# A streaming encoder step on one core: where TensorE's four attention blocks stand among the dense products of a slot

## The chip, the core and the metric

One core of a Trainium2 chip runs the whole program in one launch. The number is device time in microseconds (us), the median of three executions; a separate execution was profiled. Engines: PE is TensorE (PEld its weight loads), DVE VectorE, ACT ScalarE, POOL GpSimd, SP SyncE, which issues most of the DMAs.

## The reference

A two-layer encoder step for 1024 new frames and 64 frames of a running stream (512 past frames in a cache), width 1024, all in float32. Layer 0 projects to stick-breaking attention heads and gated spatial groups, mixes them with one output projection, and runs a SwiGLU; layer 1 has a state-space mixer, a GLU and another SwiGLU. The attention of one head is what the change touches:

```
z = einsum('bqhd,bkhd->bhqk', q, k) * HEAD_DIM**-0.5
mask = k_pos < q_pos
log_stay  = where(mask, log_sigmoid(-z), 0)
log_after = cumsum(log_stay, over keys, reverse) - log_stay
w   = where(mask, exp(log_sigmoid(z) + log_after), 0)
out = einsum('bhqk,bkhd->bqhd', w, v)
...
x = x + concat(out, gated) @ w_out
x = x + (silu(h @ w_gate) * (h @ w_up)) @ w_down
```

## The kernel before

Every dense operand is split into a high and a low part, so that a **product** is three matmuls (`three`, L248: lines 251, 252, 253) into one PSUM bank. The part of the program around the change runs from about 380 to 1000 us of the span. It is a list of **slots** (`SLOTS`, planned at L1076 to L1162). A slot holds dense groups and at most one or two **units** of attention, and each engine walks the list in order (`mid_pe`, `mid_dve`, `mid_act`, `mid_pool`, `mid_sp`).

There are 68 units. A unit is a pair of heads, one block of 128 keys and up to 512 queries: units 0 to 15 are the first 512 frames (128, 256, 384, 512 queries for the four key blocks of each head pair), units 16 to 67 the second 512 frames and the 64 running ones (per pair of heads 128, 256, 384, five times 512, then five of 64). The last unit of a group of queries has no remaining sums. PE does four things for attention:

- **sums** of unit i (`at_sums` with `tri`, L982): the running sum over keys within the block, four matmuls, after softplus and its remainder are there;
- **scores** of unit i + 3 (L970 to L974), four matmuls, two more on a diagonal block;
- **values** of unit i - 1 (L994), which read the exponent; two float32 matmuls that the trace shows as four passes;
- **remaining sums** of unit i (`at_sums` with `comp`, L982), which complete the sum for the next block of keys; they wait until DVE has subtracted the sums.

Before, a slot's PE order is sums, scores, values, in a row (`at_pe`), then half of the dense work, the remaining sums (`at_pe_rest`), and the other half.

DVE has three steps per unit: **t** (L922) subtracts the sums of unit i from its scores; **c** (L931) copies the scores of unit i + 3 out of PSUM; **s** (L939) forms the softplus of unit i + 2 and a rounding (L943) writes its high part. POOL then writes the remainder, **splo** (L955). ACT takes the exponent of unit i (L888), then three activations on the scores of unit i + 3 (L911, L913, L915) for the softplus. The buffer `tz` has four places, so c waits for the values of unit i - 1 (LEAD is 3):

```
def at_dve_c(dve, i):
    c = i + LEAD
    ...
    dve.wait_ge(sem("u_z"), c + 1)
    if c >= 4:
        dve.wait_ge(sem("u_pv"), c - 3)
    dve.tensor_copy(tz[:, c % 4, :, 0:w], ps[:, 3:5, 0:w])
```

In `mid_dve` the order in a slot is t, c, s, then the evictions of the dense groups; with four groups, t, first eviction, c, second eviction, s, the other two. Evictions are: for an up product a multiplication (L1354) and a rounding rh (L1358), after which POOL writes the remainder rl (L1325); for down, outS and outA products an addition to the residual (L1364). A gate product is evicted by ACT with silu (L1279). ACT also rounds the weight slabs (L241), POOL subtracts their remainder (L245). Dense groups use three PSUM banks in turn, so a group waits until the group three before it has been evicted (`used`).

The slots with attention are, in order: three without products that only start the pipeline; eight with one outS group of four products (units 0 to 7); nine with no product (units 8 to 16); eight with one outA group of four products (units 17 to 25); three for a norm (units 26 to 28); then the feed-forward, where a slot holds one gate group or one up group of eight products, or four down groups of two products each, in the order gate, up, gate, up, down, down (units 29 to 67). The running stream's units of 64 queries come two to a slot; the first of the two is done whole before the slot's dense work.

SP's queue holds the weight slabs and, in `at_loads` (L797), the keys, queries and values of later units, which wait for counts of scores (`u_z`) and values (`u_pv`).

Of the kernel before, what the change touches and what calls it, by code (L numbers as in the profile page):

```python
# [76 lines left out]
def build(nc, A, O):  # L77
    with ExitStack() as ctx:
        sems = {}

        def sem(name):
            if name not in sems:
                sems[name] = ctx.enter_context(nc.semaphore(name))
            return sems[name]
# [6 lines left out]
        def plan(off, *specs):  # L91

            got = []
            for name, shape, dt in specs:
                n = 4
                for s in shape[1:]:
# [16 lines left out]
        xin, nrow, _ = plan(off_g, ("xin", [P, 2, D], F32), ("nrow", [P, P], F32))  # L113
# [6 lines left out]
        ug0, _ = plan(off_end, ("ug0", [P, T], F32))  # L120
        wsr, _ = plan(off_end, ("wsr", [P, 8, P], F32))
        g4, _ = plan(off_end + T * 4, ("g4", [P, 2, GP, 4], F32))
        zhi, _ = plan(off_end, ("zhi", [P, T], F32R))
# [3 lines left out]
        zlo, _ = plan(off_g + 8 * P * 4, ("zlo", [P, T], F32R))  # L127
# [9 lines left out]
        splo, _ = plan(off_x + 4 * (2 * KCOL + 4 * 576 + 13 * P), ("splo", [P, 4, 2, 512], F32R))  # L137
# [4 lines left out]
        hA, lA, _, rh, rl, xA, mst, oa = plan(  # L142
            off_h, ("hA", [P, KD * 512], F32R), ("lA", [P, KD * 512], F32R), ("hpad", [P, 512], F32), ("rh", [P, 3, 576], F32R),
            ("rl", [P, 3, 576], F32R), ("xA", [P, KD * 512], F32), ("mst", [P, 2, 576], F32))
# [7 lines left out]
        eb, bo, co_, pb, _ = plan(off_x, ("eb", [P, 2, 8, NCH], F32), ("bo", [P, 8, 2, P], F32), ("co", [P, 8, 2, CW], F32),  # L152
                                  ("pb", [P, 2, GP, L], F32))
        zt, chi, clo, _ = plan(_, ("zt", [P, 512], F32), ("chi", [P, 512], F32R), ("clo", [P, 512], F32R))
# [5 lines left out]
        t1, t2, _ = plan(off_t, ("t1", [P, 8 * CW], F32), ("t2", [P, 8 * CW], F32))  # L160
        assert _ <= off_end
        lt, craw, lstep, _ = plan(off_t, ("lt", [P, 5, P], F32), ("craw", [P, 2, 8, 64], F32), ("lstep", [P, 2], F32))
# [6 lines left out]
        tm, kt, p4, _ = plan(off_w + 6 * D * 4, ("tm", [P, 2, 8, P], F32), ("kt", [P, 8, P], F32), ("p4", [P, 5, GP], F32))  # L169
        u, ca, sh, oa = plan(off_g, ("u", [P, 2, 8, NCH], F32), ("ca", [P, 3, 4, 2, CW], F32), ("sh", [P, 2, 2, 4, NCH], F32))  # L170
        assert oa <= off_end
        yp, _ = plan(off_h + KD * T * 4, ("yp", [P, KD * T], F32))
# [7 lines left out]
        hp, _ = plan(off_h, ("hp", [P, KD * T], F32))  # L180
        fin, fout, _ = plan(off_w - 2 * D * 4 - 3072, ("fin", [P, 4, GP], F32), ("fout", [P, 4, P], F32))
        sq, _ = plan(off_g, ("sq", [P, 6, 384], F32))
        ssum, _ = plan(off_end, ("ssum", [P, NC, 384], F32))

        yf, _ = plan(off_h, ("yf", [P, KD * T], F32))
        yo, _ = plan(off_g, ("yo", [P, 2, D], F32))
# [552 lines left out]
        NU = len(units)  # L739
# [237 lines left out]
        def at_sums(pe, i, mat):  # L977
            u, w = units[i], units[i]["w"]
            for a in range(2):
                out = ps[:, 5 + a, u["off"]:u["off"] + w]  # L980
                for j, r in enumerate((sphi[:, i % 2, a, 0:w], splo[:, i % 4, a, 0:w])):
                    mm = pe.matmul(out, mat[:], r, start=mat is tri and u["first"] and j == 0, stop=True, skip_group_check=True)  # L982
            return mm

        def at_values(pe, i):
            u, g = units[i], group_no[i]
            pe.wait_ge(sem("u_w"), i + 1)
            if u["first"]:
                v_ready(pe, i)
                if g:  # L990
                    o_taken(pe, g - 1)
            for a in range(2):
                out = ps[64 * a:64 * a + 64, 7, u["off"]:u["off"] + u["w"]]
                mm = pe.matmul(out, vv[:, u["vb"], 64 * a:64 * a + 64], tz[:, i % 4, a, 0:u["w"]],  # L994
                               start=u["first"], stop=True, skip_group_check=True)
            mm.then_inc(sem("u_pv"), 1)

        def at_pe(pe, i):
            if 0 <= i < NU:
                pe.wait_ge(sem("u_splo"), i + 1)  # L1000
                if units[i]["first"] and i:
                    pe.wait_ge(sem("u_t"), i)
                at_sums(pe, i, tri).then_inc(sem("u_tri"), 1)
            if i + LEAD < NU:
                at_scores(pe, i + LEAD)
            if 1 <= i <= NU:
                at_values(pe, i - 1)

        def at_pe_rest(pe, i):
            if 0 <= i < NU and not units[i]["last"]:  # L1010
                pe.wait_ge(sem("u_t"), i + 1)
                at_sums(pe, i, comp).then_inc(sem("u_rest"), 1)

        G, USES, SRC, SLOTS = [], {"a": 0, "v": 0}, [], []
        NORMS = [(1, 0, 0), (1, 1, 0), (1, 1, 1), (2, 0, 0), (2, 1, 0), (2, 1, 1)]
# [59 lines left out]
        for j in range(4):  # L1079
            t = slab(w_out[:, 4:8, 2 * j * P:2 * (j + 1) * P])  # L1080
            for m in (2 * j, 2 * j + 1):
                g = group("outS", 0, 0, m, [t])
# [3 lines left out]
        for j in range(4):  # L1086
            t = slab(w_out[:, 0:4, 2 * j * P:2 * (j + 1) * P])
            for m in (2 * j, 2 * j + 1):
                g = group("outA", 0, 0, m, [t])
                new_slot([g], some_steps(), sq=squares([g], (1, 0)))  # L1090
        g = group("rms", 0, 0, 0, [])
# [313 lines left out]
                        row = 8 + f  # L1405
                    dve.scalar_tensor_tensor(out, xf, cols[:, row:row + 1], rf, ALU.mult, ALU.mult).then_inc(sem("m_f"), 1)

        def dense_pe(pe, g, halfway=None):

            v = G[g]  # L1410
            kind, half, m, n, s = v["kind"], v["half"], v["m"], v["n"], v["s"]
            if g >= 3:
                used(pe, g - 3)
            out = ps[:, v["bank"], 0:n]
            for t in v["slabs"]:
                if g == min(h for h in range(max(0, g - 16), g + 1) if t in G[h]["slabs"]):
                    pe.wait_ge(sem("w_lo"), t + 1)
            if kind == "rms":
                q = rms_group.index(g)
                pe.wait_ge(sem("m_add"), q_adds[q])  # L1420
                if half == 0 and NORMS[q][0] == 1:
                    pe.wait_ge(sem("consts"), 1)
                pe.matmul(out, ones[:], msum[:, q % 2, 0:n], start=True, stop=True).then_inc(sem("g_ready"), 1)
                return
            if kind == "down":
                pe.wait_ge(sem("hid_lo"), hid_no[(half, 2 * (m_part[g]) + 1, v["c"])] + 1)
                count = 2
            else:
                count = 4 if kind in ("outS", "outA") else KD
            for j in range(count):  # L1430
                if halfway is not None and j == count // 2:
                    halfway()
                if kind == "down":
                    b = tile_no(half, 2 * m_part[g] + j) % 3
                    o = s - HALF[half][0]
                    r1, r2 = rh[:, b, o:o + n], rl[:, b, o:o + n]
                    t, col = v["slabs"][j], m * P
                else:
                    t = v["slabs"][0]
                    k, col = j, j * P  # L1440
                    if kind in ("outS", "outA"):
                        k, col = (4 + j if kind == "outS" else j), j * 256 + (m % 2) * P
                        if kind == "outS" and m == 0:
                            pe.wait_ge(sem("ms_lo"), j + 1)
                        elif kind == "outA" and m == 0:
                            pe.wait_ge(sem("o_lo"), j + 1)
                    elif kind == "outB":
                        k = (j + 4) % KD
                        col = k * P
                        if m == 0:  # L1450
                            pe.wait_ge(sem("ms_lo"), 4 + j + 1)
                    elif kind == "gate" and m == 0:
                        q = NORMS.index((1, half, v["c"]))
                        pe.wait_ge(sem("m_lo"), KD * q + j + 1)
                    r = cols_of(half, k, s, n)
                    r1, r2 = hh[half][:, r], hl[half][:, r]
                mm = three(pe, out, slot(t), col, r1, r2, j == 0, j == count - 1)
            mm.then_inc(sem("g_ready"), 1)
# [8 lines left out]
        def mid_pe(pe):  # L1467
            pe.wait_ge(sem("at_made"), 4)
            pe.wait_ge(sem("acc_used"), NC * IN_TILES)
            pe.wait_ge(sem("kv_used"), kv_taken(len(TOKS)))  # L1470
            for S in SLOTS:
                gs, at = S["groups"], S["at"]
                for i in at[:-1]:
                    at_pe(pe, i)
                    at_pe_rest(pe, i)
                for i in at[-1:]:
                    at_pe(pe, i)
                for n, g in enumerate(gs):
                    if at and len(gs) == 1:
                        dense_pe(pe, g, lambda: at_pe_rest(pe, at[-1]))  # L1480
                        continue
                    if at and n == len(gs) // 2:
                        at_pe_rest(pe, at[-1])
                    dense_pe(pe, g)
                if at and not gs:
                    at_pe_rest(pe, at[-1])

        def prep_sp(sp):  # L1490
# [890 lines left out]
```

## Time and profile before

| | us |
|---|---|
| median of three runs (lowest, highest) | 2809.38 (2804.43, 2810.51) |
| profiled execution | 2812.7 |
| its span, first to last instruction | 2810.9 |
| PE busy | 2565.4 (91% of the span) |
| PE weight loads busy | 2364.7 (84%) |
| DVE, ACT, POOL busy | 1166.2, 881.3, 1104.3 |

The mean granted TensorE clock was 0.941 of 2.4 GHz; its two levels are 1.2 and 2.4 GHz. The chain of work that ended last is PE for 75% of the span, DVE for 9%. A matmul's end is modelled, so its duration is longer than its share of PE's time: the pace is read from one start to the next. Idle time stands in brackets behind an instruction, with what ended it.

### The profile page before, as it was taken

To read this page: it belongs to the slowest core of one execution; us is meant where nothing else is said; L and a number is where in the kernel's file an instruction comes from. 1 tells how busy PE (TensorE), PEld (TensorE's weight loads), DVE (VectorE), ACT (ScalarE), POOL (GpSimd) and SP (SyncE) were. 2 spreads that over 40 slices of the span, in tenths; PEclk is the share of its full clock that TensorE was granted. 3 is DMA by queue.
4 is the path that set the end of the run, shared out by engine and by line. 5 is a ranking of instruction groups with operands and counts; after the bars stand their busy time and mean duration, and the time that the engine had idled before them with its cause. 6 is when DMAs were issued, how large, how long until landed. Compare 5 with 4: busy or idle time off the path is not lost.

```text
span 2810.9 us, 38283 instructions
## 1 busy us (share of the span) xinstructions
PE 2565.4 (91%) x15274; PEld 2364.7 (84%) x15274; DVE 1166.2 (41%) x1877; ACT 881.3 (31%) x1304; POOL 1104.3 (39%) x770
## 2 busy tenths in 40 slices
PE   6998949899997999999999587799699999999998
PEld 4898936677776978999999466799699999999998
DVE  3696637765562232422223677322412222222224
ACT  3423236788882322211221121311311111111114
POOL 2545534564454565544444200333532222222223
PEclk9999969899998999999999677899899999999999
DMA  4315664323423223322222675311011111111111
GB/s 121 103 59 198 243 200 115 86 72 82 110 72 123 83 83 98 106 83 90 76 84 68 170 195 149 126 46 46 29 40 44 41 42 44 45 45 45 45 45 64
DMA packets 290436, 254.11 MB, mean 90 GB/s; under 512 B 32561, under 2 KB 254705, under 8 KB 289025
## 3 DMA queue, kind: packets, MB, share of 16 engines
q1 hardware_dynamic: 282064, 219.96, 27.3%
q0 software_dynamic: 7088, 31.15, 2.9%
q8 instruction: 91, 1.49, 0.2%
q10 hardware_dynamic: 1152, 1.18, 0.1%
q14 instruction: 41, 0.33, 0.0%
HBM read 195.08 MB, written 54.80 MB: 89 GB/s over the span
## 4 chain that ended last, share of the span: by engine, by line
PE 75%; DVE 9%; DMA 5%; POOL 4%; ACT 2%; issue 2%; SPq 1%; POOLq 0%; DVEq 0%; ACTq 0%
PE ps L251 22%; PE ps L252 22%; PE ps L253 22%; PE ps L982 3%; PE ps L1870 1%; PE ps L994 1%; DVE v L1932 1%; DMA mst<-mT 1%; DVE fbuf L423 1%; PE ps L1868 1%; POOL hlo L431 1%; PE ps L974 1%; DVE t L1707 1%; POOL ssum L349 1%; PE ps L970 1%
## 5 line engine op out<-in xcount | busy, mean ns | idle before, releaser
L245 POOL TENSOR_TENSOR wlo<-raw,whi 128x1024 fp32r<-128x1024 f32 x250 | 602.8, 2420 | 402.1 <-ACT whi L241 400.4
L251 PE MATMUL ps<-hhi,whi 128*128 128x384 f32 (+1 forms) x1920 | 635.8, 331 | 49.0 <-POOL hlo L2019 14.9
L252 PE MATMUL ps<-hlo,whi 128*128 128x384 f32 (+1 forms) x1920 | 631.3, 329 | 0.0
L253 PE MATMUL ps<-hhi,wlo 128*128 128x384 f32 (+1 forms) x1920 | 631.1, 329 | 0.0
L251 PEld LDWEIGHTS ps<-hhi,whi 128*128 128x128 f32 x1920 | 365.2, 190 | 54.8 <-issue 22.5
L252 PEld LDWEIGHTS ps<-hlo,whi 128*128 128x128 f32 x1920 | 365.3, 190 | 0.3 <-issue 0.2
L253 PEld LDWEIGHTS ps<-hhi,wlo 128*128 128x128 f32 x1920 | 364.9, 190 | 0.0
L241 ACT ACTIVATE whi<-raw 128x1024 fp32r<-128x1024 f32 x250 | 259.1, 1054 | 312.9 <-PE ps L253 145.6
L251 PE MATMUL ps<-hB,whi 128*128 128x288 f32 x832 | 247.3, 297 | 12.3 <-POOL lB L1316 12.3
L509 POOL TENSOR_TENSOR gl<-fbuf,gh 128x384 f32 (+3 forms) x66 | 63.9, 968 | 488.8 <-DVE gh L564 488.8
L253 PE MATMUL ps<-hB,wlo 128*128 128x288 f32 x832 | 246.4, 296 | 0.0
L252 PE MATMUL ps<-lB,whi 128*128 128x288 f32 x832 | 246.2, 296 | 0.0
L561 DVE TENSOR_TENSOR fbuf<-ps,abuf 128x384 f32<-128x384 f32 (+1 forms) x66 | 35.4, 536 | 452.5 <-ACT abuf L479 448.2
L479 ACT ACTIVATE abuf<-ps 128x384 f32<-128x384 f32 (+1 forms) x66 | 31.1, 473 | 559.8 <-PE ps L253 559.8
L251 PE MATMUL ps<-rh,whi 128*128 128x288 f32 (+1 forms) x528 | 177.4, 336 | 14.7 <-DVE xA L1364 6.4
L572 DVE TENSOR_TENSOR x<-ps,x 128x384 f32<-128x384 f32 (+1 forms) x264 | 141.3, 535 | 109.9 <-PE ps L253 108.7
L1354 DVE TENSOR_TENSOR fb<-ps,ab 128x288 f32<-128x288 f32 (+1 forms) x66 | 35.3, 536 | 365.2 <-PE ps L253 342.2
L252 PE MATMUL ps<-rl,whi 128*128 128x288 f32 (+1 forms) x528 | 175.0, 332 | 0.0
L253 PE MATMUL ps<-rh,wlo 128*128 128x288 f32 (+1 forms) x528 | 174.8, 331 | 0.0
L253 PE MATMUL ps<-gh,wlo 128*128 (+2 forms) x528 | 172.1, 326 | 0.0
L252 PE MATMUL ps<-gl,whi 128*128 (+2 forms) x528 | 172.0, 326 | 0.0
L251 PE MATMUL ps<-gh,whi 128*128 (+2 forms) x528 | 172.0, 326 | 0.0
(315 smaller groups left out, 4796.6 us busy)
## 6 DMA issues: line engine op xcount, KB each, us to landing
raw<-in_ffn_w_gate SPq DMA_DIRECT2D x66, 512.0 KB, 3.8
raw<-in_ffn_w_up SPq DMA_DIRECT2D x66, 512.0 KB, 3.9
raw<-in_ffn_w_down SPq DMA_DIRECT2D x66, 512.0 KB, 3.6
raw<-in_ab_w_in SPq DMA_DIRECT2D x20, 512.0 KB, 4.1
raw<-in_ab_w_out SPq DMA_DIRECT2D x16, 512.0 KB, 3.8
raw<-in_ssm_w_glu SPq DMA_DIRECT2D x16, 512.0 KB, 3.9
dC<-co POOLq DMA_DIRECT2D x4, 1152.0 KB, 4.7
ca<-dC SPq DMA_DIRECT2D x8, 576.0 KB, 4.9
```

Of the source, the lines that this page charges most:

```text
L241: act.activation(whi[:, slot(t), :], raw[:, t % 2, :], ACT.Copy).then_inc(sem("w_hi"), 1)
L245: pool.tensor_tensor(wlo[:, slot(t), :], raw[:, t % 2, :], whi[:, slot(t), :].bitcast(F32), ALU.subtract).then_inc(sem("w_lo"), 1)
L251: pe.matmul(out, wh, rh, start=first, stop=False)
L252: pe.matmul(out, wh, rl, start=False, stop=False)
L253: return pe.matmul(out, wl, rh, start=False, stop=last)
L349: pool.tensor_tensor(ssum[:, c, 0:n], ssum[:, c, 0:n], sqbuf(k, a)[:, 0:n], ALU.add).then_inc(sem("n_add"), 1)
L479: act.activation(abuf[:, v % 2, 0:n], ps[:, 2 * (v % 2), 0:n], ACT.Silu).then_inc(sem("pair_act"), 1)
L509: pool.tensor_tensor(gl[:, bass.ds(o, n)], fbuf[:, v % 2, 0:n], gh[:, bass.ds(o, n)].bitcast(F32), ALU.subtract).then_inc(sem("hid_lo"), 1)
L561: dve.tensor_tensor(fbuf[:, v % 2, 0:n], ps[:, 2 * (v % 2) + 1, 0:n], abuf[:, v % 2, 0:n], ALU.mult).then_inc(sem("pair_used"), 1)
L572: dve.tensor_tensor(xo, acc(v)[:, 0:n], xo, ALU.add).then_inc(sem("acc_used"), 1)
L982: mm = pe.matmul(out, mat[:], r, start=mat is tri and u["first"] and j == 0, stop=True, skip_group_check=True)
L1354: dve.tensor_tensor(fb2[:, h % 2, 0:n], out, ab2[:, h % 2, 0:n], ALU.mult).then_inc(sem("use_v"), 1)
```

## The change

In a slot PE does the sums, two dense products, the scores, two products, the remaining sums, two products, the values, two products. `at_pe` becomes a generator that stops twice after each block; `dense_pe` lets it go on once before each product, so a block comes before every second product. In a unit without remaining sums the values come before the fifth product. In a slot with four products the remaining sums and the values come one after the other behind the last product; in a slot without products, and for the first unit of two in a slot, the order is sums, scores, remaining sums, values with nothing between. No other engine's order is changed.

```
         def at_pe(pe, i):
+
             if 0 <= i < NU:
                 pe.wait_ge(sem("u_splo"), i + 1)
                 if units[i]["first"] and i:
                     pe.wait_ge(sem("u_t"), i)
                 at_sums(pe, i, tri).then_inc(sem("u_tri"), 1)
+                yield
+                yield
             if i + LEAD < NU:
                 at_scores(pe, i + LEAD)
-            if 1 <= i <= NU:
-                at_values(pe, i - 1)
-
-        def at_pe_rest(pe, i):
+                yield
+                yield
             if 0 <= i < NU and not units[i]["last"]:
                 pe.wait_ge(sem("u_t"), i + 1)
                 at_sums(pe, i, comp).then_inc(sem("u_rest"), 1)
+                yield
+                yield
+            if 1 <= i <= NU:
+                at_values(pe, i - 1)
...
-        def dense_pe(pe, g, halfway=None):
+        def dense_pe(pe, g, side):
...
             for j in range(count):
-                if halfway is not None and j == count // 2:
-                    halfway()
+                next(side, None)
...
             for S in SLOTS:
                 gs, at = S["groups"], S["at"]
                 for i in at[:-1]:
-                    at_pe(pe, i)
-                    at_pe_rest(pe, i)
-                for i in at[-1:]:
-                    at_pe(pe, i)
-                for n, g in enumerate(gs):
-                    if at and len(gs) == 1:
-                        dense_pe(pe, g, lambda: at_pe_rest(pe, at[-1]))
-                        continue
-                    if at and n == len(gs) // 2:
-                        at_pe_rest(pe, at[-1])
-                    dense_pe(pe, g)
-                if at and not gs:
-                    at_pe_rest(pe, at[-1])
-
+                    for _ in at_pe(pe, i):
+                        pass
+                side = at_pe(pe, at[-1]) if at else iter(())
+                for g in gs:
+                    dense_pe(pe, g, side)
+                for _ in side:
+                    pass
```

## Rows read from the trace of the kernel before

**Rows 1.** Stretches: us; busy (count) of PE, PEld, DVE, ACT, POOL; clock; DMA

```profile
458.00:493.00 35.00, 29.44 (x158) 20.45 (x157) 26.28 (x37) 26.48 (x39) 15.91 (x10) 0.95 0.53 118
493.00:540.00 47.00, 45.76 (x221) 33.38 (x222) 39.01 (x44) 33.32 (x45) 30.51 (x18) 1.00 0.35 85
...
575.00:860.00 285.00, 282.43 (x1373) 220.90 (x1372) 167.40 (x210) 243.91 (x281) 142.00 (x81) 0.98 0.32 87
```

**Rows 2.** Timeline of PE, unit 46's slot: start, us, engine, line, operation, count

```profile
704.74 0.39 PE L982 MATMUL ps<-sphi,tri 128*128 128x512 f32 x1
...
705.64 0.39 PE L970 MATMUL ps<-qS,kS 128*128 128x512 f32 x1
...
706.64 1.08 PE L994 MATMUL ps<-tz,vv 128*64 128x512 f32 x4
707.65 0.50 PE L251 MATMUL ps<-hA,whi 128*128 128x512 f32 x1
...
710.51 0.39 PE L982 MATMUL ps<-sphi,comp 128*128 128x512 f32 x1
...
714.13 0.39 PE L982 MATMUL ps<-sphi,tri 128*128 128x512 f32 x1
```

**Rows 3.** Timeline of DVE, the same slot

```profile
705.84 1.22 DVE L922 TENSOR_TENSOR tz<-tz,ps 128x1024 f32<-128x1024 f32 x1 [2.86 <-PE ps L982]
707.84 1.23 DVE L931 COPY tz<-ps 128x1024 f32<-128x1024 f32 x1 [0.77 <-PE ps L994]
...
711.68 0.69 DVE L943 CAST sphi<-esp 128x1024 fp32r<-128x1024 f32 x1 [0.24 <-PE ps L982]
...
715.12 0.43 DVE L1358 CAST rh<-fb 128x512 fp32r<-128x512 f32 x1
```

**Rows 4.** Waits, 380 to 880: who <- whom: us in total, times, longest

```profile
DVE tz L931 <- PE ps L994: 32.8, 44, 2.4
...
PE ps L994 <- ACT tz L888: 2.1, 2, 1.3
```

**Rows 5.** Timeline of DVE, 598 to 604

```profile
599.64 1.22 DVE L939 SCALAR_TENSOR_TENSOR esp<-tz,esp 128x1024 f32<-128x1024 f32 x1
```

**Rows 6.** DVE by line and shape, 380 to 880: count, busy us, mean ns, idle before

```profile
L939 DVE SCALAR_TENSOR_TENSOR esp<-tz,esp 128x1024 f32<-128x1024 f32 x24 | 42.7, 1781 | 0.1
...
L943 DVE CAST sphi<-esp 128x1024 fp32r<-128x1024 f32 x24 | 22.0, 918 | 10.3 <-PE ps L982 9.9
...
L931 DVE COPY tz<-ps 128x128 f32<-128x128 f32 x20 | 5.8, 288 | 6.5 <-PE ps L994 6.5
```

**Rows 7.** Timeline of all engines, 587.1 to 588.2, an up slot (unit 30)

```profile
587.16 2.40 POOL L955 TENSOR_TENSOR splo<-esp,sphi 128x1024 fp32r<-128x1024 f32 x1 [0.63 <-DVE sphi L943]
...
587.23 0.69 DVE L1354 TENSOR_TENSOR fb<-ps,ab 128x512 f32<-128x512 f32 x1
...
587.96 1.88 DVE L1358 CAST rh<-fb 128x512 fp32r<-128x512 f32 x1
```

**Rows 8.** Timeline of ACT, unit 46's slot

```profile
710.16 1.05 ACT L911 ACTIVATE esp<-tz 128x1024 f32<-128x1024 f32 x1
...
713.62 1.06 ACT L915 ACTIVATE esp<-esp 128x1024 f32<-128x1024 f32 x1
```

**Rows 9.** Timeline of PE, unit 17's slot

```profile
496.06 0.44 PE L994 MATMUL ps<-tz,vv 128*64 128x128 f32 x4 [0.97 <-DVE lA L948]
```

**Rows 10.** Timeline of PE, units 39 and 40, two to a slot

```profile
649.96 0.19 PE L982 MATMUL ps<-sphi,tri 128*128 128x64 f32 x1
...
654.55 0.48 PE L994 MATMUL ps<-tz,vv 128*64 128x64 f32 x4 [1.32 <-ACT tz L888]
654.97 0.80 PE L251 MATMUL ps<-hA,whi 128*128 128x512 f32 x1
```

**Rows 11.** Stretches of 4 us, columns as in rows 1

```profile
652.00:656.00 4.00, 2.68 (x18) 2.18 (x18) 1.39 (x4) 3.92 (x6) 2.76 (x2) 0.72 0.00 0
656.00:660.00 4.00, 4.00 (x11) 3.14 (x10) 0.43 (x1) 3.91 (x7) 0.00 (x0) 0.50 0.75 223
```

## Prediction

> **What bounds the kernel now.** I read the busy time by stretch first [rows 1]. From 575 to 860 us, where nearly every slot carries eight dense products beside attention, TensorE (PE) is busy 282.4 of 285.0 us at a granted clock of 0.98; ScalarE (ACT) has 243.9, VectorE (DVE) 167.4. From 493 to 540, with four products a slot, PE has 45.8 of 47; from 458 to 493, with none, 29.4 of 35. PE runs in program order, so whatever it waits in these slots is added to the end. Then one slot at full width, unit 46, on PE [rows 2]: sums at 704.74, scores 705.64, values 706.64, first product 707.65, remaining sums 710.51, next slot 714.13. That is 9.39 us, without a wait: blocks of four 512-column matmuls take 0.90 (0.225 each), values 1.01, a dense product (three matmuls) 0.68. Then the same slot on DVE [rows 3]: the subtraction t starts at 705.84, when the sums are done. The copy c of unit 49's scores starts at 707.84, 1.20 after the values started, because it overwrites the buffer of four that the values of unit 45 read. Over the stage that wait occurs 44 times and makes 32.8 us of DVE idle [rows 4]. It harms nothing, since it falls early in the slot.
>
> **The change, part by part.** No instruction is added or removed; the matmuls, weight loads and waits are the same. The sums stay first. The scores move back by two products (1.36 us); their reader c now waits for something later anyway: 0. The remaining sums come 4.5 us into the slot (0.90 + 1.36 + 0.90 + 1.36) in place of 5.8, so t has 1.3 us less. The values go from 1.9 us into the slot to 6.8, behind six products. This last is the costly part: c (unit i+3) waits for them, and behind c in DVE's order are softplus s and the rounding of unit i+2, evictions, and t of unit i+1, for which PE's remaining sums of i+1 wait. A loop closes once per slot, with V the start of the values.
>
> PE from V to the next remaining sums, full width: values 1.01 + two products 1.47 (the first of six matmuls costs 0.11 more, 707.65 behind values) + sums 0.90 + 1.36 + scores 0.90 + 1.36 = 7.0 us. A narrower unit (384, 256, 128, 64 columns) takes less in proportion, an estimate.
>
> DVE from V to the end of t: values seen 1.20, c 1.23, s, rounding, evictions, t 1.22. For s the trace has two prices: 1.22 with GpSimd (POOL) idle [rows 5] and 1.78 in the mean [rows 6]; for the rounding 0.69 [rows 3] and 0.92 in the mean [rows 6]. I take 1.91 for the two together, the free ones, since POOL's weight subtraction would mostly fall before s, and keep 2.70 as the upper end. 64-column units take 0.29 for c [rows 6].
> - Slot with a gate product: nothing else. 1.20 + 1.23 + 1.91 + 1.22 = 5.6, covered by 7.0: 0.
> - Slot with an up product: the product's multiplication (0.69 [rows 7]) and its rounding rh (0.43 [rows 3]) now come before t, right when POOL starts splo. There rh took 1.88 instead of 0.43 and ended 0.3 us after splo's 2.40 [rows 7], so 2.7 us from rounding to t. Before s, ACT's silu of the gate slot delays POOL by about 0.5 (my estimate from ACT's chain of 4.5 us [rows 8] plus silu, slab and POOL's turn). Sum 1.20 + 1.23 + 0.5 + 1.91 + 2.7 + 1.22 = 8.8, that is 1.7 us of stall. With each unit's own widths: units 30, 32, 34, 42, 46, 56, 60: 1.5, 1.6, 1.1, 0.6, 1.7, 1.5, 1.1 = **9.1**. Below: 0 (no meeting with POOL); above: 15 (the mean prices, 0.8 more in each).
> - Slot with four down products: one eviction (0.69) before s, two after. Bank reuse makes the next slot's products wait for these too. Units 43, 44, 57, 58: 1.0, 0.6, 0.9, 0.6 = **3.1** (5.7 with 2.70).
> - First units of two-unit slots have nothing between sums and remaining sums; behind down slots (units 52, 65) DVE is 1.1 late: **2.2**.
> - Slots with outA and four products (units 17 to 21): PE from V only 5.6, DVE 6.3: 0.5, 0.6, 0.6, 0.7, 0.1 = 2.5 with the free prices, 6.2 with the mean ones (0.8 more on each of four or five). POOL is busier there than behind (30.5 of 47 us against 142 of 285 [rows 1]), so I take a value between, **4.0**.
> - Slots with outS: only unit 4, between full and narrow units, is late, 1.2, and a little on unit 5: **1.5**.
> - Nine slots without products (units 8 to 16): values now follow the remaining sums, which follow t, so c starts up to 1.6 us later. Carried along DVE's order this is about 1.75 per four units: **4.0**. Right behind them, in unit 17's slot, PE waits 0.97 before the values of unit 16 [rows 9]; products now stand before them, which gives back **1.0**.
>
> What it gives: in the two-unit slot at 650 us narrow matmuls run 5 us without a product, the last 1.32 of them a wait for the exponent [rows 10]; with one more such wait it is 2.1 us [rows 4]. In the two stretches of 4 us from 652 the granted clock is 0.72 and 0.50 [rows 11]: the 1.2 GHz level for 2.2 + 4.0 us, so 3.1 us of work lost. After the change products stand in that run, and I take both as gone: **-5.2**.
>
> Sum: 9.1 + 3.1 + 2.2 + 4.0 + 1.5 + 4.0 - 1.0 - 5.2 = +17.7 us.
>
> Costed at nothing: SyncE's queue. Its loads of keys and values wait for counts of scores and values, which come up to 5 us later; weight slabs queue behind them. What hides it: these rows are needed four slots later and a slab is two slots ahead; without that cover, up to 5 us at each of some eight places. ACT: its chain starts with c, 4 us later, and is needed only at the next slot's s: 9.4 against 4.5 [rows 8].
>
> The Trainium skill (SBUF — State Buffer, Who interferes with whom) says VectorE's two-input operations and its 2-port casts share a port pair with GpSimd, held for a whole instruction. It speaks against this change, which brings rh beside splo in every up slot; by it the up slots pay their 9.1. The 587.96 row agrees, but it is the plainest of few; without interference they would pay 0, and the sum would be +8.6.
>
> **How the time stands.** The profiled execution took 2812.7 us (span 2810.9); the three runs' median is 2809.4, 3.3 below. +17.7 gives 2830.4 for an execution like it and 2827.1, said **2827**, at the median.
>
> **Rivals.**
> (a) Covered: the loop is shorter than PE's path nearly everywhere (s and rh free of POOL, t in time); up slots cost 0 and the other losses half, 6.7 (3.1, 2.2, 2.5, 1.5 and 4.0), against gains of 6.2. For it: gate slots have 1.4 us to spare. Against: the down and the product-less slots don't depend on POOL. +0.5: about 2810.
> (b) Faster, the other side: the point is whether DVE's chain stays under 7.0 us in full-width slots and is absorbed in the product-less ones. If so, only the waits before values and the 1.2 GHz stretch go, -5.2 and -1.0: about 2803. Against it: c's wait is a real one in 44 places, and moves 4.9 us back.
> (c) Wholly bound by DVE: s and roundings meet POOL in most slots. Up 15, down 5.7, outA 6.2, the rest as above, and PE in the product-less slots, already at the lower clock for part of them (0.95 in the stretch [rows 1]), falls there for longer, doubling about 1 us of remaining sums and values on the loop in some six slots: 15 + 5.7 + 6.2 + 2.2 + 1.5 + 4.0 + 6 - 6.2 = +34, about 2844.
> (d) That interleaving itself speeds PE, small weight loads hiding behind dense matmuls. Each block that gains at its entry loses at its exit, where a dense load stands behind a narrow matmul; I count it 0 and give it no chance of its own.
>
> **How the numbers follow.** Forecast 0.62 (2816 to 2838), (a) 0.14, (b) 0.07, (c) 0.17. The range of 8 in 10 reaches into (a) and (c): 2810 to 2845. Differences under 0.2% (5.6 us) can't be told from none by measurement. Faster by more is (b), 0.07; within it is (a), 0.14; slower is the forecast and (c), 0.79.
>
> **What would show it.** DVE's c should start about 1.2 us behind the values at three quarters of the slot, with its idle for values well above 32.8 us; PE should have waits before the remaining sums on t (L922) in slots behind up and down products, none behind gates; rh (L1358) should have a mean near 2 us while attention runs; the clock near 655 us should stay at the upper level. The stage from the first sums (412 us) to the last values (855 us) should be some 17 us longer, and everything behind it only shifted. Wrong I would be if PE showed no new wait on DVE (then (a) or (b)), or if the loss stood at slab loads.

## The result and the profile after

| | before | after |
|---|---|---|
| median (lowest to highest), us | 2809.95 (2804.43 to 2812.79) | 2846.68 (2841.24 to 2853.71) |
| profiled execution, its span | 2812.7, 2810.9 | 2843.5, 2841.8 |
| DVE, ACT, POOL busy | 1166.2, 881.3, 1104.3 | 1148.1, 882.6, 1102.4 |
| mean granted clock | 0.941 | 0.936 |

Over four executions of each the ratio is 1.0135 [1.0105, 1.0164]: **slower by 36.7 us**, where 17.7 were forecast and 2845 was the upper end of the range. The sign was right, the size was half, and the range missed by 1.7 us. PE, DVE, ACT and POOL are busy for about as long as before: the time lies in waits and in TensorE's clock.

The waits first, 380 to 920 us of after (who waits, for whom: us in total, times, longest). The first line answers [rows 4]:

```profile
DVE tz L931 <- PE ps L994: 184.2, 63, 5.7
...
PE ps L982 <- DVE tz L922: 34.3, 24, 6.9
...
PE ps L982 <- POOL wlo L245: 1.9, 1, 1.9
```

The copy c waited 32.8 us for the values before; now it waits 184.2, in nearly every slot. The second line is where PE pays for it: before the sums or remaining sums it waits for t, 24 times and 34.3 us. In the same stretch of before it was

```profile
PE ps L982 <- DVE tz L922: 10.2, 4, 6.2
```

so that 24.1 us of the loss stand as waits on t; the rest are smaller waits and the lower clock below. The place shows in unit 46's slot, on PE (start, us, engine, line, operation), which answers [rows 2]:

```profile
727.41 0.39 PE L982 MATMUL ps<-sphi,tri 128*128 128x512 f32 x1
...
729.68 0.39 PE L970 MATMUL ps<-qS,kS 128*128 128x512 f32 x1
...
731.95 0.39 PE L982 MATMUL ps<-sphi,comp 128*128 128x512 f32 x1
...
734.31 1.08 PE L994 MATMUL ps<-tz,vv 128*64 128x512 f32 x4
...
736.81 0.39 PE L982 MATMUL ps<-sphi,tri 128*128 128x512 f32 x1
...
742.97 0.50 PE L982 MATMUL ps<-sphi,comp 128*128 128x512 f32 x1 [1.66 <-DVE tz L922]
```

and on DVE, which answers [rows 3]:

```profile
735.51 1.23 DVE L931 COPY tz<-ps 128x1024 f32<-128x1024 f32 x1 [5.18 <-PE ps L994]
736.65 1.66 DVE L939 SCALAR_TENSOR_TENSOR esp<-tz,esp 128x1024 f32<-128x1024 f32 x1
738.34 0.69 DVE L943 CAST sphi<-esp 128x1024 fp32r<-128x1024 f32 x1
...
739.67 2.12 DVE L1359 CAST rh<-fb 128x512 fp32r<-128x512 f32 x1
741.71 1.21 DVE L922 TENSOR_TENSOR tz<-tz,ps 128x1024 f32<-128x1024 f32 x1
```

The slot's four blocks start 2.27, 2.27 and 2.36 us apart, as predicted (0.90 and 1.36, the values a little later). From the values (734.31) to the next slot's remaining sums (742.97) are 8.66 us, of which PE's own work is 7.0. On DVE c starts 1.20 behind the values, then s, the rounding, the up product's two evictions and t follow without a gap. That is the loop: values, c, s, rounding, evictions, t, remaining sums, and values again.

The stretches of after (us; busy time and count of PE, PEld, DVE, ACT, POOL; clock; DMA), shifted by what went before, stand against [rows 1] and [rows 11]:

```profile
466.40:476.40 10.00, 9.14 (x30) 6.80 (x31) 4.78 (x8) 3.62 (x8) 3.60 (x3) 0.50 1.06 244
...
501.00:548.00 47.00, 43.72 (x196) 29.88 (x194) 31.47 (x37) 30.43 (x39) 27.57 (x15) 1.00 0.29 72
...
590.00:896.00 306.00, 288.97 (x1377) 217.50 (x1376) 157.83 (x210) 244.60 (x281) 141.74 (x80) 0.98 0.30 81
...
609.80:613.20 3.40, 3.40 (x11) 2.39 (x10) 0.00 (x0) 1.04 (x2) 2.29 (x1) 0.52 0.05 5
...
676.00:680.00 4.00, 4.00 (x27) 3.51 (x27) 1.04 (x4) 3.97 (x4) 1.09 (x1) 1.00 0.00 0
```

The third line is the feed-forward: its 285 us have become 306, with 17 us of PE idle instead of 2.6. The second, with four products a slot, has PE busy 43.7 of 47 us instead of 45.8. The first line is in the slots without products: ten microseconds at the 1.2 GHz level, where before it was low for about 3.5 (0.95 in the mean of 35 [rows 1]). The fourth is a new stretch of 3.4 us at that level, in the slot of unit 31. The last is the two-unit slot that stood at 0.72 and 0.50 before: full clock now, as forecast.

To place the loss I took each unit's first sums in both traces and subtracted. The difference is -1.3 us at unit 0, -1.4 at unit 8, +7.4 at 17, 5.8 at 18, 10.8 at 24, 14.7 at 29, 24.7 at 39, 20.6 at 41, 31.5 at 61, and 36.0 at the last values: 37.3 from first to last. The stage was expected to be some 17 us longer, with everything behind it only shifted. The end of the span is 30.9 late, since what lies behind attention came out 5.1 shorter in this trace; in the traces of the kernels below it varies likewise, and I tested nothing there.

### The profile page after: what moved, and what is told of

It reads as the page before. It is cut to its first block, busy times and chain, and to the rows that moved or that the text cites. A ratio compares the mean times of both kernels' runs of the same rounds, so it can differ in the third digit from the quotient of the medians.

```text
span 2841.8 us, 38291 instructions
## 1 busy us (share of the span) xinstructions
PE 2575.3 (91%) x15274; PEld 2361.4 (83%) x15274; DVE 1148.1 (40%) x1877; ACT 882.6 (31%) x1304; POOL 1102.4 (39%) x770
## 4 chain that ended last, share of the span: by engine, by line
PE 73%; DVE 12%; DMA 5%; POOL 4%; issue 3%; ACT 2%; SPq 1%; POOLq 0%; DVEq 0%; ACTq 0%
PE ps L251 21%; PE ps L253 21%; PE ps L252 21%; PE ps L982 3%; PE ps L994 2%; PE ps L1863 1%; DVE v L1925 1%; DVE esp L939 1%; DMA mst<-mT 1%; DVE fbuf L423 1%; PE ps L1861 1%; POOL hlo L431 1%; DVE hp L1407 1%; DVE t L1700 1%; POOL ssum L349 1%
```

## The experiments

The theory: moving the values late makes c, and with it all of DVE's work behind c, part of a loop that closes once per slot through the reuse of `tz`. The rivals: the loss lies in the interleaving itself (switches between narrow and dense matmuls cost PE, the opposite of (d)); or in TensorE's clock in the slots without products. In all that follows "shift" is the start of a unit's sums, less that of before's trace.

**A fifth place for tz.** Everything of after stays; a fifth buffer, in a place that is free by then, makes c of unit i+3 wait for the values of unit i-2, one slot earlier. The control is the same edit on before.

```diff
+        def tzb(i):
+            return tz4[:] if i % 5 == 4 else tz[:, i % 5, :, :]
...
-                if c >= 4:
-                    dve.wait_ge(sem("u_pv"), c - 3)
-                dve.tensor_copy(tz[:, c % 4, :, 0:w], ps[:, 3:5, 0:w]).then_inc(sem("u_c"), 1)
+                if c == 4:
+                    dve.wait_ge(sem("ms_lo"), 4)
+                if c >= 5:
+                    dve.wait_ge(sem("u_pv"), c - 4)
+                dve.tensor_copy(tzb(c)[:, :, 0:w], ps[:, 3:5, 0:w]).then_inc(sem("u_c"), 1)
```

Every other use of tz takes its place from `tzb` too; the wait at c = 4 is for the mixer, which uses the fifth place earlier.

> The changed kernel with a fifth place for the scores buffer tz (4 KB that the mixer's staging buffer leaves free while attention runs), so that the copy c of unit i+3 waits for the values of unit i-2, done a slot before, and no longer for those of unit i-1; PE's order stays the changed one. Theory, the loop through c: the waits of PE on t in front of the remaining sums behind up and down products go, and so does the longer stretch without products; what is left is the gain (the 1.2 GHz stretch near 655 us, the waits for the exponent): about 2803 us, between 2797 and 2810. Rival, that standing between products itself costs PE (weight loads, waits at more block boundaries): still above 2830. In between, near 2820, both have a part.

Measured: 2810.08 us over 12 runs, ratio to before 1.0001 [0.9986, 1.0016]. The whole loss is gone, with after's PE order unchanged, so that the rival of a cost in the interleaving itself falls. Its waits, 380 to 920 us (in this kernel t is L926, c L937, the sums L988, the scores L980):

```profile
DVE tz L937 <- PE ps L980: 44.3, 44, 4.3
...
PE ps L988 <- DVE tz L926: 16.5, 10, 5.8
```

c waits for the scores, not for the values, and PE's waits for t fall from 34.3 us to 16.5. The expected 2803 (2797 to 2810) was just missed on the slow side: the gain near unit 40 is there (the shift falls by 4.1), but behind it the shift grows by 4.6 again, 1.4 of it at unit 57, where PE waits 1.25 us for a weight slab, and 1.6 from unit 63 to 67, in the two-unit slots; from unit 0 to the last values 1.1 of gain is left in this trace.

> The kernel before with the same fifth place. Control: both theories say that c's wait (32.8 us of DVE idle) is hidden in the old order, so the time stays at 2810 within 4 us. If it falls by more than 6, c's wait also cost something before, and what the fifth place brings to the changed kernel is not the undoing of the change alone.

Measured: 2805.02 us over 12 runs, 0.9991 [0.998, 1.0001]. With the old order the fifth place is worth nothing that can be measured. c's wait, 32.8 us in sum before, was hidden, as the prediction said of it; moved, it was not.

**Only the values back at their old place.** Sums, two products, scores and values, two products, remaining sums, four products.

```diff
             if i + LEAD < NU:
                 at_scores(pe, i + LEAD)
-                yield
-                yield
+            if 1 <= i <= NU:
+                at_values(pe, i - 1)
+            if i + LEAD < NU or 1 <= i <= NU:
+                yield
+                yield
...
-            if 1 <= i <= NU:
-                at_values(pe, i - 1)
```

> The changed kernel with the values put right behind the scores (sums, two products, scores and values, two products, remaining sums, four products). Buffers as before. Theory: c starts some 4 us earlier in the slot, DVE has 11.9 us from the values to the next remaining sums in place of 7.0, more than its longest chain (8.8 to 10): no wait of PE on t, about 2805 us (2800 to 2812). Rival of the boundaries: scores and sums still stand apart, so at least half of the loss stays, above 2825.

Measured: 2804.8 us over 10 runs, 0.999 [0.9977, 1.0002]. The waits:

```profile
DVE tz L931 <- PE ps L994: 70.8, 54, 2.6
...
PE ps L982 <- DVE tz L922: 9.3, 3, 6.2
```

c still waits for values, twice as long as before in sum, but early in the slot, and PE's waits for t are those of before. The other separations together cost nothing. Of the shift, 5.5 us are gained in this trace, 3.9 of them near unit 40; over all runs the gain is inside the uncertainty.

**Only the values moved.** Sums and scores in a row, four products, remaining sums, two products, values, two products.

```diff
                 at_sums(pe, i, tri).then_inc(sem("u_tri"), 1)
-                yield
-                yield
             if i + LEAD < NU:
                 at_scores(pe, i + LEAD)
+            if 0 <= i < NU or i + LEAD < NU:
+                yield
+                yield
                 yield
                 yield
```

> The other half alone: sums and scores in a row as in the kernel before, four products, remaining sums, two products, values, two products. Theory: DVE has the same 7.0 us from the values to the next remaining sums, so nearly all of the loss is there: about 2842 us (2832 to 2852). Rival of the boundaries: one block less stands apart, 2825 or less; if the scores' place mattered, close to 2810.

Measured: 2855.26 us, 1.0164 [1.0146, 1.0183], above the 2832 to 2852 that I gave it. The whole loss is in the values' move, and by this order some 8 us more than by after's in the medians, though the two intervals overlap. In the traces the extra is 6.7 us and lies ahead of the feed-forward: from unit 0 to unit 26 the shift grows by 20.9 where after's grows by 14.5. Why, no run shows.

**The values one product later still.**

```diff
                 at_sums(pe, i, comp).then_inc(sem("u_rest"), 1)
                 yield
                 yield
+                yield
```

> The changed kernel with the values one product later (behind the seventh in place of the sixth, in units with remaining sums and slots of eight products). Theory: PE's way from the values to the next remaining sums is one product (0.68 us) shorter and DVE's chain the same, so every slot in which PE waits on t pays 0.68 more: eleven in the feed-forward, +7.5, about 2854 us (2850 to 2859), and slots behind gates still pay nothing (5.6 against 6.3). Rival, that the loss is not this loop: within 3 us of 2847.

Measured: 2865.55 us, 1.0215 [1.0195, 1.0234]: 0.80% above after's ratio, some 22 us, where 7.5 were expected. The sign follows the theory; the total doesn't. The profiled execution was the fastest of the four, and its trace holds 13.7 us more than after's from unit 0 to the last values. The other three were not traced. The price of one wait came out as expected: each of PE's five waits on t behind up slots is 0.67 to 0.71 us longer than in after, where 0.68 was worked out. For unit 47 it is, in after and here,

```profile
742.97 0.50 PE L982 MATMUL ps<-sphi,comp 128*128 128x512 f32 x1 [1.66 <-DVE tz L922]
750.39 0.65 PE L982 MATMUL ps<-sphi,comp 128*128 128x512 f32 x1 [2.33 <-DVE tz L922]
```

Yet behind the up slots of units 46 and 60 the shift grows by 4.3 and 4.6 us instead of 2.1 and 2.5. Three of six stretches of the feed-forward at the lower clock in this kernel's trace (columns as before) show the rest of why, as far as this trace goes:

```profile
655.00:658.40 3.40, 3.40 (x10) 2.64 (x9) 0.00 (x0) 0.12 (x1) 1.58 (x1) 0.50 1.03 225
750.60:753.80 3.20, 3.20 (x8) 2.45 (x8) 0.00 (x0) 1.67 (x2) 2.29 (x1) 0.50 0.01 3
...
870.00:873.40 3.40, 2.95 (x7) 2.37 (x8) 0.39 (x1) 1.06 (x1) 2.96 (x2) 0.51 0.00 0
```

After has two such stretches there (609.8 and 811.2). With longer stalls the granted clock falls behind more of them, and then the work that follows is slower too: 3.4 us at half clock are 1.7 us more, so the four more are 6.8 us, beside the 7.5 worked out. The length of the wait alone doesn't decide: in after the wait of 2.14 us before 651.49 left the clock at full speed,

```profile
651.60:655.00 3.40, 3.40 (x15) 1.90 (x15) 0.34 (x1) 0.84 (x1) 2.32 (x1) 1.00 1.04 240
```

and so did one of 2.09 (856.65), while one of 1.87 (810.63) did not. What decides, no run shows.

**Evictions ahead of s.** In up slots DVE does the multiplication and rh between c and s, so that rh no longer runs beside splo.

```diff
                 if not at or len(gs) < 4:
                     cut1 = cut2 = 0
+                if at and [G[g]["kind"] for g in gs] == ["up"]:
+                    cut2 = 1
```

> The changed kernel, but in a slot with an up product DVE evicts that product (multiplication and rounding rh) between c and s, no longer behind s. PE's order and all waits stay. Theory: what made the up slots dear is the meeting with POOL, rh with splo (2.65 us from the rounding to t) and s with the weight remainder (s 2.7 to 3.1 us in four of the seven full-width up slots). With rh 3 us after the values start and s behind it, both are free: the chain from values to t falls from 8.6 to 9.9 to about 7.3, so 7 slots give back 1.3 to 2.5 each: 2847 - 13 = 2834 (2828 to 2840). Rival, that DVE's bare work is too long whoever meets whom: 2843 or more, because the order within DVE does not change the sum.

Measured: 2839.38 us, 1.0101 [1.0082, 1.012], inside the 2828 to 2840 around the 2834 expected. Its interval overlaps after's, so the gain is read from the traces: from unit 0 to the last values the shift grows by 26.7 us instead of 37.3. This kernel's waits and unit 46's slot on DVE:

```profile
PE ps L982 <- DVE tz L922: 23.8, 21, 6.9
```

```profile
731.28 1.23 DVE L931 COPY tz<-ps 128x1024 f32<-128x1024 f32 x1 [5.19 <-PE ps L994]
732.84 0.69 DVE L1355 TENSOR_TENSOR fb<-ps,ab 128x512 f32<-128x512 f32 x1 [0.34 <-PE ps L253]
733.57 0.43 DVE L1359 CAST rh<-fb 128x512 fp32r<-128x512 f32 x1
733.91 1.22 DVE L939 SCALAR_TENSOR_TENSOR esp<-tz,esp 128x1024 f32<-128x1024 f32 x1
...
735.77 1.22 DVE L922 TENSOR_TENSOR tz<-tz,ps 128x1024 f32<-128x1024 f32 x1
```

The instructions are the same as in after, but rh takes 0.43 instead of 2.12 and s 1.22 instead of 1.66. t ends 6.9 us behind the values (730.08 in this trace), inside PE's 7.0. The growth of the shift behind units 30, 32, 34, 46 and 60 falls from 4.6, 2.0, 2.5, 2.1, 2.5 to 0.2, 0.1, 0.7, 0.4, 0.6. So in these up slots it is the meeting with POOL that decides. The 2.0 and 2.2 between units 56 and 58 stay, and the early part stays.

**The new order only in slots of eight products.** All slots ahead of the feed-forward, and first units of two, keep the old order (`at_pe_old`).

```diff
+        def at_pe_old(pe, i):
...
-                    for _ in at_pe(pe, i):
+                    for _ in at_pe_old(pe, i):
...
+                eight = sum(2 if G[g]["kind"] == "down" else 8 if G[g]["kind"] in ("gate", "up") else 0 for g in gs) == 8
-                side = at_pe(pe, at[-1]) if at else iter(())
+                side = (at_pe if eight else at_pe_old)(pe, at[-1]) if at else iter(())
```

> The changed order only in slots with eight products (units 29 on); in slots with four or none, and for the first unit of a two-unit slot, the order of the kernel before. Theory by the shift from trace to trace: units 0 to 26 lost 12 to 14 us of the 37 (8.8 in the slots without products, 5.0 in the outA slots), so about 2833 (2828 to 2838). If the half of the clock lost in the slots without products were the main thing, more would return: 2825 or less.

Measured: 2827.85 us, 1.0067 [1.005, 1.0084]. The feed-forward's part is about 18.8 us, the other half, 17.9, lies ahead of it, where the shift is now flat between 2.1 and 2.6 up to unit 31. I had expected a little more from the feed-forward (2828 to 2838). PE waits for t 20.9 us in 9 places:

```profile
PE ps L982 <- DVE tz L922: 20.9, 9, 6.2
```

**Matmuls without use in the slots without products.** Four of 512 columns into an unused bank, between the scores and the remaining sums of units 8 to 16, to hold the clock up. They only add work.

```diff
+            if 8 <= i <= 16:
+                if i == 8:
+                    used(pe, 7)
+                for _ in range(4):
+                    pe.matmul(ps[:, 0, :], identr[:], hA[:, 4 * 512:5 * 512], start=True, stop=True)
             if 0 <= i < NU and not units[i]["last"]:
                 pe.wait_ge(sem("u_t"), i + 1)
```

> The changed kernel with four 512-column matmuls of no use between the scores and the remaining sums in the nine slots without products (units 8 to 16), where PE stands 0.8 to 2.9 us for t. They add 3.6 us of work per four units, the more part of it in idle time. If the lower clock there (13.4 us at 1.2 GHz in the changed kernel, 3.5 before) makes the stretch longer, the clock stays up and the shift over units 8 to 17, 8.8 us in the changed kernel, falls to 7 or less, the total by 1 to 3 us. If the order alone makes it, the shift stays at 8.8 or grows by up to 2.

Measured: 2850.85 us, 1.0155 [1.0136, 1.0174]. The stretches of this kernel (columns as before):

```profile
466.00:476.00 10.00, 7.36 (x42) 5.32 (x40) 7.29 (x9) 6.40 (x9) 5.58 (x3) 1.00 0.68 165
466.00:493.00 27.00, 22.26 (x122) 15.70 (x120) 18.09 (x26) 17.64 (x25) 10.16 (x6) 1.00 0.66 154
```

The clock stays at 2.4 GHz through all of it, and still the shift grows by 8.7 us from unit 8 to unit 17, against 8.8 in after. The lower clock isn't what that stretch can be won back by. It isn't excluded as a part: the added matmuls are 0.9 us a slot, and what they cost and what the clock gave are not told apart.

**Both remedies together.** Values at their old place, and five places for tz (the first and the second diff).

> Both remedies together: values right behind the scores, and the fifth place for tz. By the traces of the two alone, the values' place gives 5.5 us by the end of attention, nearly all in the two-unit slot near 650 us, and the fifth place under the old order 3.4 us in the slots without products: if they add up, 2807 - 8 = 2799 us (2796 to 2803), faster than both kernels. If the fifth place brings nothing once the values come early, 2804.

Measured: 2803.27 us over 12 runs, 0.9987 [0.9973, 1.0], the lowest median of all, but no gain that can be told from none; 2799 was expected. In the traces, from unit 0 to the last values, the shift falls by 6.4 us here, by 5.5 in values_second and 3.4 in five_before: the two gains add only in part.

## Why the prediction was half right

In the table, in us, the growth of the shift over the units of each term.

| term | predicted | measured |
|---|---|---|
| outS, units 0 to 8 | +1.5 | -0.1 |
| slots without products, 8 to 17 | +4.0 | +8.8 |
| given back at unit 17 | -1.0 | -1.6 |
| outA, 18 to 24 | +4.0 | +5.0 |
| last outA and norm slots, 24 to 29 | 0 | +3.9 |
| up slots: behind 30, 32, 34, 42, 46, 60 | +7.6 | +14.6 |
| behind the up slot of 56, and the weight slab late at unit 57 | +1.5 | +4.2 |
| down slots: behind 43, 44, 57, 58 | +3.1 | +2.2 |
| two-unit slots | +2.2 | +3.1 |
| wait for the exponent and clock, near unit 40 | -5.2 | -4.1 |
| not placed | | +1.3 |

The sum failed by the size of its terms: the up slots above all, the slots without products, and two terms put at nothing, the slots of units 24 to 29 and the late slab.

**The mechanism** was right in the main: c starts 1.20 behind the values, PE has new waits on t of 1.66 to 2.79 us behind the up slots of units 30, 32, 34, 46 and 60 and none behind gates, the lower clock near 655 us goes. Behind the down slots of units 43, 44, 57 and 58 the forecast had PE wait for t and for the banks of the dense groups; only the second is there, 0.4 us before the sums of the next unit, for an eviction:

```profile
718.11 0.50 PE L982 MATMUL ps<-sphi,tri 128*128 128x512 f32 x1 [0.40 <-DVE xA L1365]
```

five_after and values_second remove the loss through two different links of the loop, values_only brings it alone, values_later deepens it. Rivals (a) and (b) needed DVE's chain inside PE's 7.0 us; it is 8.66 in unit 46's slot. Of (d), a gain by interleaving itself, no run shows a measurable one: where the loop's loss is gone, the ratios are 1.0001 (five_after) and 0.999 (values_second).

**The step that failed in the up slots** is the price of s: "I take 1.91 for the two together, the free ones, since POOL's weight subtraction would mostly fall before s". All engines of after around unit 30's up slot, 601 to 610 us:

```profile
601.47 2.40 POOL L245 TENSOR_TENSOR wlo<-raw,whi 128x1024 fp32r<-128x1024 f32 x1 [4.11 <-ACT whi L241]
...
601.83 3.13 DVE L939 SCALAR_TENSOR_TENSOR esp<-tz,esp 128x1024 f32<-128x1024 f32 x1
...
605.76 2.36 POOL L955 TENSOR_TENSOR splo<-esp,sphi 128x1024 fp32r<-128x1024 f32 x1 [1.89 <-DVE sphi L943]
...
606.32 2.09 DVE L1359 CAST rh<-fb 128x512 fp32r<-128x512 f32 x1
...
608.33 0.94 DVE L922 TENSOR_TENSOR tz<-tz,ps 128x768 f32<-128x768 f32 x1
...
609.33 0.44 PE L982 MATMUL ps<-sphi,comp 128*128 128x384 f32 x1 [2.79 <-DVE tz L922]
```

POOL's subtraction started only 0.36 us ahead of s and still had 2.0 us to run. s took 3.13 us and ended 1.09 behind wlo, that is, nearly its whole own 1.22 after POOL let go. With its rounding it is 3.82 where 1.91 and a delay of 0.5 stood in the sum: 1.4 more. PE's wait is 2.79, 1.3 more than the 1.5 forecast for this slot; behind units 34 and 60 it is 2.14 and 2.09, where 1.1 stood for each. Most of the rest of the 4.6 us at unit 30's place is the clock: 0.52 for the 3.4 us behind the wait, 1.6 us of work. s met POOL so in four of the seven up slots (2.7 to 3.1 us in units 30, 34, 56, 60). In unit 46's slot it took 1.66, and there DVE's predicted 8.8 stands against 8.66 measured. Had I taken the nearest upper price, the mean of 1.78 [rows 6], it would still have been short: a mean over 24 slots held both kinds. In after that mean has even fallen (DVE by line and shape, 380 to 920: count, busy us, mean ns):

```profile
L939 DVE SCALAR_TENSOR_TENSOR esp<-tz,esp 128x1024 f32<-128x1024 f32 x24 | 39.7, 1656 | 0.0
...
L943 DVE CAST sphi<-esp 128x1024 fp32r<-128x1024 f32 x24 | 16.7, 694 | 0.8
```

In the gate slots of units 31 and 33 s took 3.16 and 3.05 us before and 1.22 after; in the up slots of units 30, 34 and 56 it took 1.22 before and 3.13, 2.75 and 3.08 after. So in these slots the change took s away from POOL where it cost nothing and put it beside POOL in the loop.

**rh beside splo** was right. Of the nine roundings between 606 and 813 us the median is 2.09 us (shortest, median, longest in ns), as the forecast of "near 2" said; from the end of the rounding to t it is 2.65 to 2.68 in the up slots of units 30, 32, 34, 46, 56 and 60, where 2.7 stood in the sum:

```profile
L1359 DVE CAST rh<-fb x9: 427/2090/2122, 606.3 to 812.9; 128x512 fp32r<-128x512 f32 x9
```

The Trainium skill (SBUF — State Buffer, Who interferes with whom) has it that VectorE instructions with two SBUF inputs, and 2-port casts, contend with GpSimd for a shared port pair, and that an instruction with at most one SBUF input, outside the 2-port modes, doesn't. The trace agrees on all three: s 3.13 instead of 1.22, rh 2.09 instead of 0.43, and t, whose other input is in PSUM, 1.21 as ever, also where POOL's splo had started 1.03 us ahead of it (721.03). I had weighed this rule for rh alone; by it s had to be asked the same question.

**The slots without products** cost 8.8 instead of 4.0, and rival (c) gave them 10 by the lower clock. The clock was indeed low for 13 us there (466.4 to 476.4 and 486.8 to 490), but keep_busy, at full clock, is no better. How the 8.8 divide stays open; that they come with the new order in the early slots, eight_only shows. **The slots of units 24 to 29** I had not costed at all: I counted outA only up to unit 21 and the norm slots as nothing. They go in eight_only as well. In the traces PE's waits for the norm there are longer, 3.9 us instead of 2.8 and 6.9 instead of 6.2; what makes them longer was not tried.

**ACT costed at nothing** was wrong at one place. ACT, POOL, DVE and PE of after, ahead of unit 57:

```profile
806.93 1.05 ACT L241 ACTIVATE whi<-raw 128x1024 fp32r<-128x1024 f32 x1
...
808.06 2.36 POOL L245 TENSOR_TENSOR wlo<-raw,whi 128x1024 fp32r<-128x1024 f32 x1 [4.11 <-ACT whi L241]
...
808.43 3.08 DVE L939 SCALAR_TENSOR_TENSOR esp<-tz,esp 128x1024 f32<-128x1024 f32 x1
...
810.63 0.41 PE L982 MATMUL ps<-sphi,tri 128*128 128x384 f32 x1 [1.87 <-POOL wlo L245]
```

ACT's chain starts with c, so the slab that it rounds afterwards comes later, POOL's remainder behind it, and PE stands 1.87 us before the sums, put down to POOL. The next 3.4 us are at the 1.2 GHz level, which makes most of the 2.2 us of shift that follow: s met POOL in this slot too, but PE has no wait on t behind it. evict_first, where s is free there, leaves both losses where they were, as it moves nothing of that chain.

**The number of rival (c)**, 2844, is near the result, but not for all of its reasons. Its up slots (15) and outA (6.2) are near 14.6 and 5.0, its down slots (5.7) are not (2.2), its clock term isn't borne out by keep_busy, and it lacks the norm slots and the late slab: that the total is so near is in part luck. My chance of 0.17 for it was too small: it asked of s in every up slot what the sum asked of rh.

## What to carry to other kernels

A wait that falls in an idle stretch of an engine costs nothing until the work that ends it is moved; before moving a consumer later, follow who must refill its buffer, add up that engine's chain until it comes back to the moved block, and compare with the time that the bounding engine has between. One more buffer, or the consumer left where it was, took this loop away. Price each instruction of the chain by its meeting with another engine at its new time: a mean over all slots mixes met and unmet ones.

## What the runs showed of the hardware that was not expected

- A VectorE operation with two SBUF inputs of 1024 columns took 1.22 us alone and 3.13 when GpSimd's subtraction had started 0.36 us earlier; it ended 1.09 us behind it.
- TensorE's clock fell to 1.2 GHz for 3.4 us behind a wait of 2.79 us (609.8) and one of 1.87 us (811.2), but not behind waits of 2.14 us (651.49) and 2.09 us (856.65): the length of one wait doesn't decide. A product later for the values gave six such stretches in the feed-forward instead of two; the loss grew by 13.7 us in the trace and by some 22 over all runs, where 7.5 were worked out.
- Three orders of the same matmuls with the values in the late part of the slot differ by up to 0.8% (ratios to before of 1.0135, 1.0164 and 1.0215; the intervals of the first two overlap).
